# Forget-gate recurrence in one block: four state products side by side, nine groups of modulation products inside and a fifth one ahead of it

## The reference, cut to what matters

```
state = 0
for t in tokens:
    state = exp(logf[t])[:, None] * state + k[t][:, None] * v[t]
    out[t] = q[t] @ state
```

## Time and profile before

| what | us |
|---|---|
| median of 3 runs (3592.45 to 3594.01) | 3593.79 |
| the profiled execution's time | 3587.6 |
| its span, first to last instruction | 3585.9 |
| mean granted TensorE clock | 0.947 of full |
| the stage of `hgrn_heads` and `end_aside` | about 2564.5 to 2668.6 |

### The profile page before, as it was taken

The page is one execution under the profiler, slowest core; times in us unless marked ns, Lnnn a source line. Parts: engine busy times, 40 slices in busy tenths (PEclk is TensorE's granted clock), DMA queues, the critical chain, the costliest instruction groups (busy, mean ns, idle before and its releaser), DMA issues. The chain is left out here.

```text
span 3585.9 us, 54305 instructions
## 1 busy us (share of the span) xinstructions
PE 3289.4 (92%) x20646; PEld 2841.2 (79%) x20646; DVE 2146.1 (60%) x4081; ACT 1456.4 (41%) x2274; POOL 41.7 (1%) x66
## 2 busy tenths in 40 slices
PE   6987899999999898999999999699889999979897
PEld 4844799998888677999997888488656787867797
DVE  4523489875777735699776788523673433244553
ACT  3312444444555434444444555323333332233443
POOL 0000000000000000000000000000120000000000
PEclk8988999999999999999999999799997999979999
DMA  5575576556888644676657787432453332321453
GB/s 186 157 237 191 183 219 202 173 177 186 242 242 242 197 130 153 195 206 183 176 176 222 242 242 241 133 96 65 166 193 96 102 99 88 94 61 52 123 166 123
DMA packets 225065, 596.61 MB, mean 166 GB/s; under 512 B 27424, under 2 KB 97440, under 8 KB 224576
## 3 DMA queue, kind: packets, MB, share of 16 engines
q1 hardware_dynamic: 220656, 588.17, 53.8%
q10 hardware_dynamic: 4176, 5.29, 0.5%
HBM read 558.16 MB, written 35.19 MB: 165 GB/s over the span
## 5 line engine op out<-in xcount | busy, mean ns | idle before, releaser
L2528 PE MATMUL ps<-h_split,split_layer 128*128 128x256 f32 x6144 | 773.1, 285 | 10.9 <-DVE split_layer L2317 10.9
L2528 PEld LDWEIGHTS ps<-h_split,split_layer 128*128 128x128 f32 x6144 | 746.5, 192 | 14.2 <-DVE split_layer L2317 14.2
L2674 PE MATMUL ps<-split_layer,h_split 128*128 128x512 f32 x3072 | 702.1, 391 | 13.9 <-DVE h_split L2658 13.9
L2674 PEld LDWEIGHTS ps<-split_layer,h_split 128*128 128x128 f32 x3072 | 580.4, 189 | 135.2 <-DVE split_layer L2641 14.3
L800 PE MATMUL ps<-h_parts_ffn,split_ffn 128*128 128x512 f32 (+1 forms) x2112 | 380.6, 341 | 21.2 <-DVE h_parts_ffn L273 12.0
L800 PEld LDWEIGHTS ps<-h_parts_ffn,split_ffn 128*128 128x128 f32 x2112 | 329.6, 191 | 73.7 <-issue 23.1
L2317 DVE TENSOR_TENSOR split_layer<-ring,split_layer 128x1024 fp32r<-128x1024 f32 x256 | 311.6, 1219 | 79.6 <-ACT split_layer L2456 78.0
L742 DVE TENSOR_TENSOR split_ffn<-ring,split_ffn 128x1024 fp32r<-128x1024 f32 x132 | 161.1, 1225 | 255.9 <-ACT split_ffn L724 247.1
L2641 DVE TENSOR_TENSOR split_layer<-ring,split_layer 128x1024 fp32r<-128x1024 f32 x256 | 313.7, 1225 | 0.0
L2464 ACT ACTIVATE kept_layer<-ps 128x256 f32<-128x256 f32 x256 | 98.4, 384 | 459.0 <-PE ps L2528 458.9
L2623 ACT ACTIVATE split_layer<-ring 128x1024 fp32r<-128x1024 f32 x256 | 267.5, 1045 | 4.5 <-PEq L485 4.5
(11 more groups left out here) (590 smaller groups left out, 3782.5 us busy)
## 6 DMA issues: line engine op xcount, KB each, us to landing
ring<-in_experts SPq DMA_DIRECT2D x512, 512.0 KB, 3.8
ring<-in_mod SPq DMA_DIRECT2D x96, 512.0 KB, 4.7
ring<-in_ada SPq DMA_DIRECT2D x96, 512.0 KB, 4.3
ring<-in_ffn_in SPq DMA_DIRECT2D x88, 512.0 KB, 3.6
hidden_layer<-kept_layer SPq DMA_DIRECT2D x256, 128.0 KB, 2.0
x_sb<-hidden_layer SPq DMA_DIRECT2D x256, 128.0 KB, 3.8
ring<-in_ffn_out SPq DMA_DIRECT2D x44, 512.0 KB, 3.6
ring<-in_peer_q SPq DMA_DIRECT2D x32, 512.0 KB, 3.6
```

The source lines that it names most:

```text
L2528: ins = nc.tensor.matmul(ps[:, 4 + j % 2, 0:T], w[:, part, c], self.hsplit[:, moving, k, :], start=(k == 0 and n == 0), stop=(k == KT - 1 ...
L2674: ins = nc.tensor.matmul(ps[:, 2 * t + h, :], wsplit(j, a)[:, t * P:(t + 1) * P], w[:, b, h * 512:(h + 1) * 512], start=(j == 0 and n == 0 ...
```

## The change

- `hgrn_heads` is one block for all eight items; its engines meet only at its end, and pass work by semaphores of their own (eight new ones).
- VectorE: scan and mid subtraction of item n + 1, then one masked copy for all four tiles of item n, then its chain. The clearing of `att` is gone: two `att` tensors, one for each direction, are cleared once by GpSimd. The second subtraction and the product of `e_last` with the keys move to GpSimd.
- GpSimd: five instructions an item in place of three.
- TensorE: sums are made in token form. `att` and the 32 columns of `e_b` of a chunk are the weights, the values and the state are the moving columns; four chunks of a tile go to four strips of 32 partitions of the bank. Their order is 3, 4, 4 and 4 chunks, each group with one wait for its last state. Each head's sums are moved by ScalarE, turned back by four transposes and moved again.
- Modulation products: one group ahead of item 0, one in each item, nine in all; the mLSTM hosts a fifth one ahead of its last totals and moves its fourth row itself. `end_aside` has only the wait left.

The core of the diff (removed lines are those of the kernel above):

```diff
@@ hgrn_heads
+            @block.gpsimd
+            def _(pool):
+                for d in range(2):
+                    ins = g.memset(att[d], 0.0)
+                ins.then_inc(cleared.sem, 1)
+                for t, (h, d) in enumerate(items):
+                    pool.wait_ge(scanned.sem, at[scanned] + t + 1)
...
+                    g.tensor_tensor(ch(e_last), wide(last[d]), ch(b), ALU.subtract).then_inc(lasts.sem, 1)
+                    pool.wait_ge(exps.sem, at[exps] + 5 * t + E_INV)
+                    g.tensor_tensor(e_inv, e_inv, k(h, d), ALU.mult).then_inc(factored.sem, 1)
+                    pool.wait_ge(exps.sem, at[exps] + 5 * t + E_LAST)
+                    g.tensor_tensor(e_last, e_last, k(h, d), ALU.mult).then_inc(factored.sem, 1)
+                    pool.wait_ge(exps.sem, at[exps] + 5 * t + E_MID)
+                    g.tensor_tensor(e_mid, e_mid, q(h), ALU.mult).then_inc(factored.sem, 1)
+                    g.tensor_tensor(e_b, e_b, q(h), ALU.mult).then_inc(factored.sem, 1)
...
+                front(0)
+                for n in range(N):
+                    if n + 1 < N:
+                        front(n + 1)
+                    choose(n)
+                    chain(n)
...
+                exponentials(0)
+                for n in range(N):
+                    h, d = items[n]
+                    keys(n)
+                    if d == 0 and h:
+                        keep_sums(h - 1)
+                    if n + 1 < N:
+                        exponentials(n + 1)
+                    if d == 0 and h:
+                        keep_head(h - 1)
+                    self.keep_row(act, first + n)
+                keep_sums(HEADS - 1)
+                keep_head(HEADS - 1)
+                self.keep_row(act, first + N)
...
+                for j in range(first, first + G):
+                    self.fetch_group(sp, j)
+                    self.store_row(sp, j)
...
+                def values(n):
+                    pe.wait_ge(masked.sem, at[masked] + n + 1)
+                    for j in range(NT):
+                        ins = nc.tensor.matmul(ps[:, 6, tile(j)], att[d][:, tile(j)], value[:, j, h * P:(h + 1) * P],
+                                               start=(d == 0 and j == 0), stop=False, skip_group_check=True)
...
+                def carry(n, c0, c1):
+                    if c0 == 1:
+                        pe.wait_ge(factored.sem, at[factored] + 4 * n + F_B)
+                    pe.wait_ge(states.sem, at[states] + STEPS * n + c1 - 1)
+                    for c in range(c0, c1):
+                        ins = nc.tensor.matmul(ps[rows(o[c]), 6, tile(o[c] * HCHUNK // P)],
+                                               e_b[:, o[c] * HCHUNK:(o[c] + 1) * HCHUNK], state[:, o[c - 1], :], start=False,
+                                               stop=(d == 1 and c == NC - 1), skip_group_check=True)
...
+                self.aside_products(pe, 8 * first, 8 * first + 8)
+                turn_keys(0)
+                scores(0)
+                for n, (h, d) in enumerate(items):
+                    aside = 8 * (first + 1 + n)
+                    update(n)
+                    if d == 0 and h:
+                        turn_head(h - 1)
+                    values(n)
+                    self.aside_products(pe, aside, aside + 4)
+                    carry(n, 1, 4)
+                    carry(n, 4, 8)
+                    self.aside_products(pe, aside + 4, aside + 8)
+                    if n + 1 < N:
+                        turn_keys(n + 1)
+                    carry(n, 8, 12)
+                    carry(n, 12, NC)
+                    if n + 1 < N:
+                        scores(n + 1)
+                turn_head(HEADS - 1)
@@ mlstm, tensor
                     totals(2 * h, range(2, NT))
+                self.aside_products(pe, 8 * (hosted0 + HEADS), 8 * (hosted0 + HEADS) + 8)
                 totals(N - 1, range(NT))
@@ mlstm, scalar
+                    self.keep_row(act, hosted0 + h)
                     if h + 1 < HEADS:
-                        self.keep_row(act, hosted0 + h)
                         weigh(2 * h + 2)
@@ mlstm, sync
-                    if h + 1 < HEADS:
-                        self.store_row(sp, hosted0 + h)
-        self.groups_hosted(hosted0, HEADS)
+                    self.store_row(sp, hosted0 + h)
+                self.fetch_group(sp, hosted0 + HEADS)
+        self.groups_hosted(hosted0, HEADS + 1)
```

More of the change, by code:

```diff
@@ L3058, in hgrn_heads @@
         nc, ps, A = self.nc, self.ps, self.arena
-        v, s = nc.vector, nc.scalar
-        NC = TA // HCHUNK
-        NT = TA // P
+        v, s, g = nc.vector, nc.scalar, nc.gpsimd
+        NC, NT = TA // HCHUNK, TA // P
+        STEPS = NC - 1
         items = [(h, d) for h in range(HEADS) for d in range(2)]
-        b, att, ktok = (self.hT[:, i, :] for i in range(3))
+        N = len(items)
+        b, ktok, att, kept = self.hT[:, 0, :], self.hT[:, 2, :], [self.hT[:, 1, :], self.hT[:, 3, :]], self.hT[:, 5, :]
         state = A.take(NC, P)
@@ L3069, in hgrn_heads @@
         tile = lambda j: slice(j * P, (j + 1) * P)
+        tiled = lambda x: x.rearrange("p (a t) -> p a t", t=P)
         rows = lambda c: slice(c * HCHUNK % P, c * HCHUNK % P + HCHUNK)
         upd = lambda c: ps[:, 2 + c % 4, c // 4 * P:(c // 4 + 1) * P]
[L3073 to L3206 removed]
@@ new lines, in hgrn_heads @@
+        backward = list(range(NC // 2 - 1, -1, -1)) + list(range(NC - 1, NC // 2 - 1, -1))
+        order = [list(range(NC)), backward]
+        mid, last = [HCHUNK // 2 - 1, HCHUNK // 2], [HCHUNK - 1, 0]
+        way = [lambda x: x, lambda x: x[:, ::-1]]
+        cleared, scanned, mids, lasts = self.cleared, self.scanned, self.mids_made, self.lasts_made
+        exps, factored, scored, turned, ktok_done = self.exps, self.factored, self.c, self.d, self.f
+        updates, masked, states, valued, contributed = self.g, self.e, self.states_made, self.valued, self.contributed
@@ new lines, in hgrn_heads @@
+        self.n_used += 4 * G
+        self.products_at += 8 * G
+        self.to_keep = []
+        self.row_moved.up(G), self.row_stored.up(sum(16 * self.jobs[j][3] for j in range(first, first + G)))
+        for x, n in ((cleared, 1), (scanned, N), (mids, N), (lasts, N), (exps, 5 * N), (factored, 4 * N), (scored, N),
+                     (turned, N), (ktok_done, N), (updates, N), (masked, N), (states, STEPS * N), (valued, N),
+                     (contributed, N), (sums_moved, HEADS), (sums_turned, HEADS), (head_moved, HEADS)):
+            x.up(n)
```

237 lines of the change are left out of this document (123 added, 114 removed).

## The result

The first comparison gave 3565.34 us (median of 4, 3563.54 to 3571.57) against 3593.12 for the kernel before (median of 4, 3588.01 to 3594.01), a ratio of 0.9929 with a 95% interval of 0.9911 to 0.9946. The prediction of 3577.7 was 12 us too high, and its range of 3570 to 3587 began 5 us above the measured median: the sign was right, the size was not. All timed runs of the study together, on several chips: 16 of the changed kernel, mean 3567.1, and 41 of the one before, mean 3588.1. That is **-21.0 us**, give or take 2.9 (two standard errors of the difference; one execution scatters by 5 us either way). The means of the three comparisons by themselves differ by 25.6, 18.0 and 23.4.

The account below looks back on a forecast made before the run. VectorE's chain was taken to bound the recurrence stage, 104.1 us of a kernel mostly TensorE matmuls. Terms -13.0 - 0.4 - 4.4 + 1.7 = -16.1 us, from 3593.8 to 3577.7 us; range 3570 to 3587.

Parts of the forecast that it names:

- carrying the 6.2 us between the profiled execution and the median over: Whole kernel: the shown median lay 6.2 us above the profiled execution, so 3571.5 became 3577.7 us.
- Seven periods: Recurrence stage, chain start to chain start: four of 8.3 and three of 8.85 us, 59.8 against 72.8, -13.0 us.
- the walk: TensorE's and ScalarE's steps through an item, timed from a state chain's end: periods of 8.85 us in items 2, 4, 6.
- The state products side by side: TensorE, each item: four products of a state in four 32-partition strips take 0.28 us a group.
- The masked copy: VectorE, each item: one copy of 512 columns takes 0.70 us, bounds 0.6 and 0.89, and runs beside GpSimd.
- The port: VectorE and GpSimd, each item: operations with two SBUF operands exclude GpSimd's one at a time, 8.27 us together.
- Rival 1: VectorE's chain, all items but the last: GpSimd's subtraction adds 1.27 us, periods of 9.55, time 3583.5 us; chance 0.19.
- The opening: From the mLSTM's end to the first chain: 12.6 us, 1.0 of it for a lower clock, against 13.0, -0.4 us.
- The end: Behind the last state chain, to the next stage: 8.25 us, 4.1 for stores landing, against 12.7, -4.4 us.
- The mLSTM: The fifth group ahead of the mLSTM's last weighted totals makes them start 1.7 us late, bounds 0.5 and 3.
- rival 4: Recurrence stage: row moves and scores fit under every chain, cold opening free, periods of 8.2, -20, 3573.5 us; chance 0.10.
- rival 3: TensorE, each item: the four state products run one after another, periods 10.5 and 11.6, time 3597 us; chance 0.05.

## Why the prediction was wrong, and where it was right

**The step that failed first is the last one: carrying the 6.2 us between the profiled execution and the median over.** The sum was made against the profiled execution (3587.6) and gave 3571.5; the pooled mean of the changed kernel is 3567.1. The three runs that made the median of 3593.8 were a high draw of a kernel whose 41 runs have a mean of 3588.1, and the four of the result were a low draw of the changed one. This accounts for 5.7 of the 12.4 us (3593.8 less 3588.1); 4.9 are the size of the gain, and 1.8 the result's own draw (3567.1 less 3565.3). That the profiled execution's own time lay near the mean is luck: those of the changed kernel lie 4.5, 6.5 and 8.1 above its mean.

**The second is a term put at nothing: the stages behind.** The prediction counts what is edited and lets the rest stay. The same code behind the recurrence takes 2.2, 5.7 and 5.2 us less up to the kernel's end. The edited stretches came to -18.1, -17.1 and -18.5 against the -16.1, close in part because the errors of the end and the mLSTM have opposite signs.

**The terms.** The size is -21.0 measured against -16.1:

- *Seven periods*: -13.0 forecast, -13.5 to -14.1 measured. The 8.3 of items 1, 3, 5 and 7 was close for a reason that the prediction did not give. It took VectorE's own list for what sets it; that list, forecast at 8.29, takes 8.05 when nothing is waited for, and TensorE's steps behind the last state set 8.38, as the run with early scores shows. The 8.85 for items 2, 4 and 6 was wrong: the row is out 4.9 us after the chain's end and not 5.75, half of that because GpSimd's subtraction ends at 2.75 and not 3.2, the rest because ScalarE's instructions start closer together than the walk had them. The scores start at 8.8 and not 9.5; between the two the walk's 3.75 us stand (3.9 in the trace). With the row move early the period stayed 8.38.
- *The state products side by side*: 0.28 forecast, 0.42 from first to last record, some 0.35 start to start. The rival that they run one after another fell with the first row.
- *The masked copy*: 0.70 forecast, 0.73. It runs beside GpSimd's subtraction (2599.82 inside 2599.25 to 2600.79), and neither is stretched by it: the subtraction takes 1.54 here, and the same 1.54 in the opening, where only the mid subtraction stands beside it. The rule of the Trainium skill (SBUF — State Buffer, Who interferes with whom) that one SBUF input does not take part agrees with the trace.
- *The port*: VectorE's mid subtraction takes it first (0.69) and GpSimd's, released by the same scan, takes 1.54 instead of the 1.04 that it needs alone. Rival 1 did not happen: all of VectorE's instructions in an item keep their times. In the opening the two do stretch each other, 1.85 and 1.57 for VectorE, as the walk had it.
- *GpSimd's subtraction*: 1.27 taken, 1.04 alone. The repeated operand costs nothing there either.
- *The opening*: -0.4 forecast, -0.6 to -0.9. At full clock under scores and updates it is 10.6, where the walk without its allowance had 11.55; the clock cost 1.5 to 1.8 and not 1.0. The two errors cancel in part.
- *The end*: -4.4 forecast, -6.2 to -7.0. This is the edited stretch most in error. I took the 4.1 us between the stores and the next stage over as the stores' own time. It was the loads ahead of them in the DMA queues; in the changed kernel those were issued sooner, and 2.2 us were left.
- *The mLSTM*: +1.7 forecast, +3.2, outside the bound of 3. I let the second half follow the data too soon: loading was to stop near 2558.8 in the time of the kernel before, and the last unit was used at 2564.4, which is 2560.1 there. Its units are issued from 2555.6 to 2557.4, and TensorE gets the third of them at 2563.1 and the fourth at 2564.4, some 7 us after their issue, with waits of 1.47 and 0.19 us for the ring.
- *Not in the sum*: the next 150 us, same code, gain 2.8, 5.9 and 5.6 against the one trace of the kernel before. This goes with the clock granted there. I give it for the next stage's first 10.8 us after its first ScalarE instruction, and for the 20 us from 82 us on. The kernel before has 0.69 and 0.58, the changed one 0.84 and 0.58, 0.84 and 0.67, 0.82 and 0.67. The other nine traces agree: the two more with 0.67 in the second stretch gain 5.4 and 5.0, the five with 0.63 or 0.64 gain 3.1 to 3.5, the one with 0.77 and 0.59 gains 1.5, and the kernel with the stores ahead, 0.70 and 0.58, gains nothing. So a stretch behind the edit can gain or lose several us by how TensorE arrives in it. Which instruction before it decides was not tried, nor whether the kernel before always gets the lower clock, since it has a single trace here.
- *Rivals*: rival 4 (-20) is nearest in size, but only its first half happened: row moves and scores fit in all items, while the clock in the opening did cost. In rival 3 four periods of 10.5 and three of 11.6 make 76.8 and not 77.8, so that its time by its own terms is 3594.7 and not 3597; it did not happen.

The range did not allow for the base. The terms' own errors, -0.8, -0.4, -2.1 and +1.5 in the mean, and the -4.4 of the stages behind would have left 3571.5, still inside it.

## What to carry to other kernels

A time between two events at the end of a stage belongs to what the events wait for: ask of a store or a barrier which loads were issued ahead of it before its wait is taken over into another schedule. When a list on one engine is made lighter, look at the chain on the next engine between two of its stretches as well: here 0.4, 1.0 and 1.2 us of TensorE work behind each chain's end set the period, and moving one of them ahead of the last state freed 0.3 us an item. And where single executions scatter by 5 us, a difference below 10 is read from stretches of two traces, and the base of a forecast needs more than three executions: here it was off by 5.7 us, a quarter of the whole gain.

## What had not been expected of the hardware

- One execution differs from another by up to 12 us within the first 420 us of identical code (1.3 to 13.3 against the kernel before), and by at most 4.1 us more in the 2000 us after that.
- The opening takes 1.5 to 1.8 us more where scores and updates run at the lower clock (2.06 to 2.08 and 1.71 to 2.08 in place of 1.16 and 1.17). The mean clock of the stretch does not tell it: 10.6 us were measured at 1.00 and at 0.84. Nor does the longest idle time of TensorE: the clock stayed at 1.00 behind 2.90 us, and fell where the longest was 1.77.
- Two stores of 8 KB behind four 512 KB loads kept the next stage waiting 5.0 us after the end of their issue; issued ahead of the loads, 2.9 us, in both kernels that have that order.
